# Scales before shifts: the first adaptive layer of a diffusion block is loaded in two halves

## Chip, cores and metric

The kernel runs on one core of a Trainium2 chip. The metric is the time of one launch on the device in microseconds (us), median over runs.

## What is computed

One block over 256 latent tokens and 256 context tokens of width 2048, all in fp32. What matters here is its beginning:

```
mod   = silu(c) @ ada_w + ada_b            # 6 x 2048 columns: sh1, sc1, g1, sh2, sc2, g2; the same for c_ctx
h     = rms_norm(x, norm1_g) * (1 + sc1) + sh1
hc    = rms_norm(ctx, norm1_g) * (1 + csc1) + csh1
proj  = h @ w_in                            # q, k, v of two attentions (8 heads each), then gates
projc = hc @ w_in                           # k, v of the context
```

Two attentions, a gated merge with an output projection and a gated ConvFFN follow; the change leaves them alone, but for the places at which the rest of `ada_w` (columns 4096 and up, 16 groups of 512 columns) is summed beside them.

## The kernel before

**Exact products from rounded halves.** A weight chunk (two 128-row blocks by 512 columns, 512 KB) lands in one of 8 slots of `raw`. ScalarE rounds it into `w_hi` (round_hi, L680), VectorE writes the rest into `w_lo` (split_lo, L1147); both have 4 slots. TensorE multiplies high by high, high by low and low by high (L1811 to L1813 for keys, L1882 to L1885 for q, L1899 to L1901 for v). Activations are stored transposed and split in the same way in `hT`, by 16 column blocks kc. A projection job is 8 slots of 4 tiles; a q job needs latent tokens alone and so fewer columns. Jobs 0 to 5 are k, q, v, q, k, v of the first attention, then comes that attention, then jobs 6 to 11 for the second. A slot can be rounded again once TensorE has used it (`used`), so ScalarE and VectorE can be up to four slots ahead.

**The head.** SP loads, in the order of the list HEAD, 64 chunks of `ada_w` (for one kc, 512 shift and 512 scale columns) in four quarters of 16, and among them the 8 chunks of the first key weights into the `ada_raw` buffers. A unit (unit_ada, L1794) multiplies one such chunk by the pair (c, c_ctx): four fp32 products of 256 columns at four partition offsets (L1803). When a quarter is summed, ScalarE reads the row sums (L746), TensorE turns them into columns (turn_mod, L1783), and VectorE makes gain and shift for four kc (modulation1, L1179). For each kc TensorE turns the normalised tokens (turn_tokens, L1770), ScalarE scales and shifts them in one activation per stream (modulate, L754) and VectorE splits the result (split_modulated, L1201). K_TILES says after which unit each (slot, tile) of the key job, here called a piece, is issued: six products of two kc. Keys of quarter q run behind the units of quarter q + 1, the last two slots after all units. The q job follows (L2010).

**The rest of the adaptive layer.** GpSimd loads 16 groups of 512 columns, 8 chunks of two kc each, into the four `ada_raw` buffers (load_ada, L596). VectorE adds one kc at a time to an accumulator (ada_step, L1208, line L1222). ADA_STEPS says how many of these 256 steps go with which job, ADA_SPAN over which slots; a job's VectorE order is, per slot, the chunk's low half, then the steps. TensorE adds up each group's partitions with four products of 128 columns (sum_mod, L1867, line L1872). Loads of group g, pair p, wait until VectorE has done step 16g + 2(p - 3). The first group waits for `mod1_ready` = 4, that is for the last quarter's gain.

Every engine works its instructions in order. SP's queue, GpSimd's queue and ScalarE's queue are three queues of transfers on the same 16 DMA engines.

Of the kernel before, what the change touches and what calls it, by code (L numbers as in the profile page):

```python
# [23 lines left out]
P = 128  # L24
# [57 lines left out]
K_AFTER = (3, 10)  # L82


K_TILES = {(0, 0): (1, 6), (0, 1): (1, 8), (0, 2): (1, 10), (0, 3): (1, 12),
# [5 lines left out]


def head_units():

    units = [("ada", 0, kc) for kc in range(KC)]
    for q in range(1, QUARTERS):
        for kc in range(KC):
            units += [("k", 2 * q - 2 + n) for n in range(2) if K_AFTER[n] == kc]
            units.append(("ada", q, kc))
    return units + [("k", 2 * QUARTERS - 2), ("k", 2 * QUARTERS - 1)]  # L100
# [3 lines left out]
ADA_UNITS = [unit for unit in HEAD if unit[0] == "ada"]  # L104
ADA_BANKS = (0, 4, 5, 4)
# [3 lines left out]
MOD_BANK = 6  # L109


def loads_before(j):

    return len(ADA_UNITS) // SLOTS + j
# [96 lines left out]
def block_program(nc, x, c, ctx, c_ctx, ada_w, ada_b, norm1_g, w_in, na_rpb, diff_lambda, diff_norm_g,  # L211
# [28 lines left out]
    tokens = place("tokens", arena, [P, 2 * TOK, D])  # L240
    modulated = place("modulated", arena + 32 * kb, [P, 4, 2, SEQ])
# [55 lines left out]
    shift1 = keep("shift1", [P, 2, KC])  # L297
# [31 lines left out]
    with ExitStack() as es:  # L329
# [19 lines left out]
        exp_c_ready = sem("exp_c_ready")  # L349
        start_dve = sem("start_dve")  # L350
        ones_ready = sem("ones_ready")
# [3 lines left out]
        lam_exp = sem("lam_exp")  # L355
        lam_ready = sem("lam_ready")
# [13 lines left out]
        k_landed = sems("k_landed", 2)  # L370
# [144 lines left out]
        def _(sp):  # L515
# [9 lines left out]
            shift_scale = ada_w[0][:, 0:2 * D].rearrange("(k p) (b n) -> p k b n", p=P, b=2)  # L525
            for kind, *unit in HEAD:
                if kind == "ada":
                    q, kc = unit
# [5 lines left out]
                else:  # L534
                    s, = unit
                    if s >= 2:
                        sp.wait_ge(lo_ready[s - 2], 1)
# [1783 lines left out]
```

## Time and profile before

| | us |
|---|---|
| median of 3 runs | 1720.55 (1719.09 to 1721.94) |
| the profiled execution | 1720.02 |
| its span, first to last instruction | 1718.3 |
| TensorE busy, share of span | 1677.8, 98% |
| VectorE, ScalarE busy | 1086.3, 752.6 |

All times in the rows are microseconds from the start of the span, durations too, unless marked ns. PE is TensorE, PEld its weight loads, DVE VectorE, ACT ScalarE, POOL GpSimd, SP SyncE. L1803 is a line of the kernel. PEclk is the granted clock as a share of 2.4 GHz. A product's duration on the timeline overlaps the next; its cost in a stream is the difference of two starts.

### The profile page before, as it was taken

What the parts mean: (1) busy time and instruction counts of PE and PEld (TensorE: products, weight loads), DVE (VectorE), ACT (ScalarE), POOL (GpSimd) and SP (SyncE); (2) the same over time, 40 slices, a digit from 0 to 9 for tenths busy, and PEclk for the clock granted to TensorE, in tenths of its full rate; (3) what the DMA queues carried; (4) which work ended last, traced back from release to release, by engine and by line L of the source; (5) the groups of instructions that cost most, each with busy time, mean ns of one, the idle gap of its engine ahead of it and who ended that gap; (6) DMA issues with size and microseconds to landing.
All of it is one profiled execution on the core that took longest, in us unless ns stands there. A gap on an engine that the chain in (4) does not pass through costs nothing.

```text
span 1718.3 us, 23725 instructions
## 1 busy us (share of the span) xinstructions
PE 1677.8 (98%) x8768; PEld 1371.5 (80%) x8768; DVE 1086.3 (63%) x1366; ACT 752.6 (44%) x962; POOL 108.6 (6%) x161
## 2 busy tenths in 40 slices
PE   4999999999999999999999999999999999999997
PEld 1568888888888678888888788888888888888886
DVE  1338787768887674554555666666666666655556
ACT  2233321623222664444444555555555555544444
POOL 0002222122121000000000000000000000000000
PEclk7999999999999999999999999999999999999999
DMA  9999888269896128566565566666666665655552
GB/s 353 386 387 347 298 296 297 79 215 328 259 321 200 52 90 271 191 189 191 192 234 195 148 190 190 188 191 188 191 187 191 185 184 188 202 195 194 191 193 83
DMA packets 161813, 371.47 MB, mean 216 GB/s; under 512 B 11671, under 2 KB 12423, under 8 KB 160598
## 3 DMA queue, kind: packets, MB, share of 16 engines
q1 hardware_dynamic: 140240, 291.65, 52.5%
q0 software_dynamic: 20144, 74.22, 12.7%
q10 hardware_dynamic: 1366, 4.74, 0.7%
q8 instruction: 41, 0.67, 0.2%
q14 instruction: 22, 0.18, 0.0%
HBM read 368.36 MB, written 2.21 MB: 216 GB/s over the span
## 4 chain that ended last, share of the span: by engine, by line
PE 94%; DMA 3%; DVE 1%; issue 0%; ACT 0%; SPq 0%; DVEq 0%; POOL 0%; ACTq 0%
PE ps L1885 21%; PE ps L1884 11%; PE ps L1899 10%; PE ps L1901 10%; PE ps L1900 10%; PE ps L2253 5%; PE ps L2252 5%; PE ps L2254 5%; PE ps L1811 4%; PE ps L1813 3%; PE ps L1812 3%; DMA raw<-in_ada_w 3%; PE ps L1882 1%; PE ps L1803 1%; PE ps L1968 1%; PE ps L1950 1%
## 5 line engine op out<-in xcount | busy, mean ns | idle before, releaser
L1147 DVE TENSOR_TENSOR w_lo<-raw,w_hi 128x1024 fp32r<-128x1024 f32 x480 | 584.5, 1223 | 419.7 <-ACT w_hi L680 419.2
L680 ACT CAST w_hi<-raw 128x1024 fp32r<-128x1024 f32 x480 | 503.4, 1050 | 763.3 <-PE ps L1885 271.2
L1885 PE MATMUL ps<-h2T,w_hi 128*128 128x512 f32 x1320 | 462.7, 394 | 0.0
L1884 PE MATMUL ps<-h2T,w_lo 128*128 128x256 f32 x1320 | 366.8, 278 | 0.0
L1885 PEld LDWEIGHTS ps<-h2T,w_hi 128*128 128x128 f32 x1320 | 247.8, 188 | 53.7
L1884 PEld LDWEIGHTS ps<-h2T,w_lo 128*128 128x128 f32 x1320 | 248.2, 188 | 3.9
L1899 PE MATMUL ps<-w_hi,hT 128*128 128x512 f32 x512 | 201.7, 394 | 0.0
L1901 PE MATMUL ps<-w_hi,hT 128*128 128x512 f32 x512 | 199.4, 389 | 0.0
L1900 PE MATMUL ps<-w_lo,hT 128*128 128x512 f32 x512 | 199.3, 389 | 0.0
L1222 DVE SCALAR_TENSOR_TENSOR ada_acc<-ada_raw,silu_c,ada_acc 128x512 f32<-128x512 f32 x240 | 179.9, 750 | 29.4 <-DMA ada_raw<-in_ada_w 14.1
L603 POOL DMA_DIRECT2D ada_raw<-in_ada_w x128 | 91.2, 712 | 381.5 <-DVE ada_acc L1222 226.4
L1899 PEld LDWEIGHTS ps<-w_hi,hT 128*128 128x128 f32 x512 | 96.1, 188 | 21.2 <-issue 1.9
L1901 PEld LDWEIGHTS ps<-w_hi,hT 128*128 128x128 f32 x512 | 96.1, 188 | 20.3
L2252 PE MATMUL ps<-w_hi,f_hi 128*128 128x512 f32 x288 | 112.0, 389 | 0.0
L2253 PE MATMUL ps<-w_lo,f_hi 128*128 128x512 f32 x288 | 112.0, 389 | 0.0
L2254 PE MATMUL ps<-w_hi,f_lo 128*128 128x512 f32 x288 | 112.0, 389 | 0.0
L1900 PEld LDWEIGHTS ps<-w_lo,hT 128*128 128x128 f32 x512 | 96.2, 188 | 19.1
L1811 PE MATMUL ps<-hT,w_hi 128*128 128x512 f32 x256 | 103.9, 406 | 1.0 <-DVE hT L1205 1.0
L1813 PE MATMUL ps<-hT,w_lo 128*128 128x512 f32 x256 | 100.0, 390 | 0.0
L1812 PE MATMUL ps<-hT,w_hi 128*128 128x512 f32 x256 | 99.9, 390 | 0.0
L1885 PE MATMUL ps<-hT,w_hi 128*128 128x512 f32 x240 | 84.2, 393 | 0.0
L1884 PE MATMUL ps<-hT,w_lo 128*128 128x256 f32 x240 | 67.3, 280 | 0.0
(231 smaller groups left out, 1985.6 us busy)
## 6 DMA issues: line engine op xcount, KB each, us to landing
raw<-in_ffn_w_up SPq DMA_DIRECT2D x176, 512.0 KB, 3.8
raw<-in_w_in SPq DMA_DIRECT2D x152, 512.0 KB, 4.8
ada_raw<-in_ada_w POOLq DMA_DIRECT2D x128, 512.0 KB, 5.9
raw<-in_ffn_w_down SPq DMA_DIRECT2D x88, 512.0 KB, 4.3
raw<-in_ada_w SPq DMA_DIRECT2D x64, 512.0 KB, 10.4
raw<-in_w_out SPq DMA_DIRECT2D x32, 512.0 KB, 4.4
raw<-in_w_branch_a SPq DMA_DIRECT2D x16, 512.0 KB, 3.6
raw<-in_w_branch_b SPq DMA_DIRECT2D x16, 512.0 KB, 3.6
```

The lines of the kernel that those rows point to most:

```text
L680: act.copy(w_hi[:, s % SPLIT_SLOTS, :], raw[:, s, :]).then_inc(hi_ready[s], 1)
L1147: dve.tensor_tensor(w_lo[:, s % SPLIT_SLOTS, :], raw[:, s, :], w_hi[:, s % SPLIT_SLOTS, :], ALU.subtract).then_inc(lo_ready[s], 1)
L1222: dve.scalar_tensor_tensor(acc, raw_columns, silu_c[:, kc:kc + 1], acc, ALU.mult, ALU.add).then_inc(ada_summed, 1)
L1811: pe.matmul(o, w_hi[:, row4(slot), at], hT[:, :, 0, kc, :], start=(kc == 0), stop=False)
L1884: pe.matmul(ps[:, b + t, 0:SEQ], w_lo[:, row4(s), at], high(kc), start=False, stop=False)
L1885: return pe.matmul(o, w_hi[:, row4(s), at], both(kc), start=False, stop=(kc == KC - 1))
L1899: pe.matmul(ps[:, b, :], hi, w_hi[:, row4(s), at], start=(kc == 0), stop=False)
L1900: pe.matmul(ps[:, b, :], hi, w_lo[:, row4(s), at], start=False, stop=False)
L1901: mm = pe.matmul(ps[:, b, :], lo, w_hi[:, row4(s), at], start=False, stop=(kc == last))
L2252: pe.matmul(ps[:, b, :], hi, w_hi[:, row4(s), at], start=start, stop=False)
L2253: pe.matmul(ps[:, b, :], hi, w_lo[:, row4(s), at], start=False, stop=False)
L2254: return pe.matmul(ps[:, b, :], lo, w_hi[:, row4(s), at], start=False, stop=stop)
```

## The change

Scales and shifts are loaded apart. There are 8 groups of 8 chunks: groups 0 to 3 hold the scales of the four quarters, groups 4 to 7 the shifts; a chunk now holds two kc by 512 columns of one kind, and a unit (unit_mod) is again four products of 256 columns, with the two kc of a chunk at different partition offsets. VectorE therefore adds the two halves when it makes a gain or a shift.

After each scale quarter, ScalarE multiplies the turned tokens by the gain alone and writes them back over `tokens` (scale_tokens); VectorE splits these into `hT` (split_scaled), and keys are computed from scaled tokens without the shift. When a shift group is there, and a key slot has been used, ScalarE adds the shift to the kept scaled tokens and rounds it into `hT` (shift_hi), VectorE writes the low half (shift_lo). The q job (head_q) uses these; its weights too are loaded in the head, through `ada_raw`. Its units of the last two shift groups stand after its slots 1 and 4, the turns after slots 2 and 5.

What the keys lack is shift @ w_k, one vector each for latent and context tokens. GpSimd loads the 8 chunks of key weights a second time (load_fix, into the place of the tokens), each behind one pair of adaptive group 1; after slot 4 of job 2 TensorE waits for all eight and multiplies them by the shifts (fix_products, 64 products of 128 columns), turns the row after slot 6 (turn_fix), and VectorE, after the low half of slot 7, adds the vector to the keys (fix_k) before that slot's adaptive steps. Job 3 waits for `k_bias`.

The token loads move from ScalarE's queue to SP's: x first of all, ctx behind ident, c and c_ctx. The `modulated` buffers go. GpSimd's first adaptive group waits for `hT_ready` = 32, all shifted activations. ADA_STEPS is redrawn: job 1 has none, 112 steps instead of 128 come before the first attention.

```diff
-ADA_STEPS = {1: 12, 2: 34, 3: 13, 4: 37, 5: 32, 6: 24, 7: 13, 8: 28, 9: 13, 10: 32, 11: 18}
+ADA_STEPS = {2: 36, 3: 13, 4: 35, 5: 28, 6: 28, 7: 13, 8: 34, 9: 15, 10: 36, 11: 18}
+MOD_BANKS = (4, 5, 4, 5, 4, 5, 0, 1)
 def head_units():
+    units = []
+    for q in range(QUARTERS):
+        units += [("mod", q, i) for i in range(SLOTS)]
+        units += [("w", 2 * q), ("w", 2 * q + 1)]
+    for q in range(2):
+        units += [("mod", QUARTERS + q, i) for i in range(SLOTS)]
+    units += [("w", SLOTS + n) for n in range(4)]
+    units += [("mod", QUARTERS + 2, i) for i in range(SLOTS)]
+    units += [("w", SLOTS + 4), ("w", SLOTS + 5)]
+    units += [("mod", QUARTERS + 3, i) for i in range(4)]
+    units += [("w", SLOTS + 6)]
+    units += [("mod", QUARTERS + 3, i) for i in range(4, SLOTS)]
+    return units + [("w", SLOTS + 7)]
...
@@ sync
+            sp.dma_start(tokens[:, 0:TOK, :], x[0].rearrange("(t p) n -> p t n", p=P)).then_inc(tokens_landed, 16)
...
+            sp.dma_start(tokens[:, TOK:2 * TOK, :], ctx[0].rearrange("(t p) n -> p t n", p=P))\
+                .then_inc(ctx_landed, 16)
...
+                    if n >= SLOTS:
                         sp.wait_ge(ada1_used, n - SLOTS + 1)
...
+                    if u >= ADA_SLOTS:
+                        sp.wait_ge(lo_ready[(u - ADA_SLOTS) % SLOTS], (u - ADA_SLOTS) // SLOTS + 1)
+                    sp.dma_start(ada_raw[:, u % ADA_SLOTS, :, :], w_in_v[:, 2 * s:2 * s + 2, col:col + GROUP])\
+                        .then_inc(head_landed[u % ADA_SLOTS], 16)
...
@@ gpsimd
-            pool.wait_ge(mod1_ready, QUARTERS)
+            pool.wait_ge(hT_ready, 2 * KC)
             load_ada(0, skip_wait=True)
...
-            pool.wait_ge(hT_ready, KC)
-            load_ada(1, between=load_first_bias)
+            def load_fix(pair):
+                pool.dma_start(fix_w[pair][:].rearrange("p (a n) -> p a n", a=2),
+                               w_in_v[:, 2 * pair:2 * pair + 2, KA:KA + GROUP])\
+                    .then_inc(fix_landed, 16)
+
+            def load_first(pair):
+                load_fix(pair)
+                load_first_bias(pair)
+
+            load_ada(1, between=load_first)
...
@@ scalar (after the scale quarters)
+            read_mod_rows(QUARTERS)
+            head_hi(SLOTS)
+            for kc in range(2):
+                shift_hi(kc)
+            read_mod_rows(QUARTERS + 1)
+            for kc in range(2, 4):
+                shift_hi(kc)
+            head_hi(SLOTS + 1)
+            for kc in range(4, 6):
+                shift_hi(kc)
+            read_result(JOB_NA)
+            for kc in range(6, 8):
+                shift_hi(kc)
+            head_hi(SLOTS + 2)
+            head_hi(SLOTS + 3)
+            read_mod_rows(QUARTERS + 2)
+            head_hi(SLOTS + 4)
+            for kc in range(8, 10):
+                shift_hi(kc)
+            head_hi(SLOTS + 5)
+            for kc in range(10, 12):
+                shift_hi(kc)
+            read_mod_rows(QUARTERS + 3)
+            for kc in range(12, 14):
+                shift_hi(kc)
+            head_hi(SLOTS + 6)
+            for kc in range(14, KC):
+                shift_hi(kc)
+            head_hi(SLOTS + 7)
...
@@ vector
+            def fix_k():
+                dve.wait_ge(mod_cols_ready, MOD_GROUPS + 1)
+                turned = ps[:, FIX_TURNED_BANK, 0:P].rearrange("p (a w) -> p a w", w=32)
+                dve.tensor_copy(k_bias[:], turned[:, :, 0:2]).then_inc(mod1_ready, 1)
+                dve.wait_ge(mod1_ready, MOD_GROUPS + 1)
+                dve.wait_ge(kv_read, 1)
+                keys = kT[:, 0:TILES, :].rearrange("p a (s n) -> p a s n", s=2)
+                dve.tensor_tensor(keys, keys, k_bias[:].unsqueeze(3).to_broadcast([P, TILES, 2, SEQ]), ALU.add)\
                     .then_inc(mod1_ready, 1)
...
+                    split_lo(j, s)
+                    if (j, s) == (FIX_JOB, SLOTS - 1):
+                        fix_k()
...
@@ tensor
+            for i in range(SLOTS):
+                unit_mod(0, i)
+            turn_tokens(0)
+            turn_mod(0)
+            turn_tokens(1)
+            pe.wait_ge(vecs_ready, 3)
+            for q in range(QUARTERS - 1):
+                for n in range(2 * TILES):
+                    s, t = 2 * q + n // TILES, n % TILES
+                    head_k(s, t)
+                    if n in (0, 1):
+                        turn_tokens(SHARE * q + 2 + n)
+                    if n < 4:
+                        unit_mod(q + 1, 2 * n)
+                        unit_mod(q + 1, 2 * n + 1)
+                    if n == 3:
+                        turn_tokens(SHARE * (q + 1))
+                    if n == 4:
+                        turn_mod(q + 1)
+                    if n == 5:
+                        turn_tokens(SHARE * (q + 1) + 1)
+            for n in range(2 * TILES):
+                s, t = SLOTS - 2 + n // TILES, n % TILES
+                head_k(s, t)
+                if n in (0, 1):
+                    turn_tokens(KC - 2 + n)
+                    for i in range(4):
+                        unit_mod(QUARTERS, 4 * n + i)
+                if n == 2:
+                    turn_mod(QUARTERS)
+                if n in (3, 4):
+                    for i in range(4):
+                        unit_mod(QUARTERS + 1, 4 * (n - 3) + i)
+                if n == 6:
+                    turn_mod(QUARTERS + 1)
...
+            for s in range(SLOTS):
+                head_q(s)
+                if s in (1, 4):
+                    for i in range(SLOTS):
+                        unit_mod(QUARTERS + (2 if s == 1 else 3), i)
+                if s == 2:
+                    turn_mod(QUARTERS + 2)
+                if s == 5:
+                    turn_mod(QUARTERS + 3)
...
+            def fix_between(s, t):
+                if (s, t) == (4, TILES - 1):
+                    fix_products()
+                if (s, t) == (6, TILES - 1):
+                    turn_fix()
+
+            projection(FIX_JOB, fix_between)
+            pe.wait_ge(mod1_ready, MOD_GROUPS + 1)
+            for j in range(FIX_JOB + 1, JOB_DIFF - 1):
                 projection(j)
```

## Rows read from the trace of the kernel before

**Rows 1.** The page: busy us, share of the span and instructions of each engine.

```profile
PE 1677.8 (98%) x8768; PEld 1371.5 (80%) x8768; DVE 1086.3 (63%) x1366; ACT 752.6 (44%) x962; POOL 108.6 (6%) x161
```

**Rows 2.** Busy us (count) by stretch; PEclk, DMA share and GB/s last.

```profile
0.00:34.00 34.00, 13.35 (x103) 0.77 0.94 344
34.00:52.00 18.00, 15.12 (x114) 0.59 1.05 387
...
52.00:112.00 60.00, 59.81 (x472) 33.54 (x469) 16.83 (x29) 14.26 (x24) 0.00 (x0) 0.99 1.05 387
...
131.00:153.00 22.00, 22.00 (x127) 19.21 (x126) 19.68 (x24) 10.15 (x9) 7.05 (x10) 1.00 1.02 349
...
164.00:174.00 10.00, 10.00 (x51) 7.86 (x51) 9.25 (x12) 2.11 (x2) 3.10 (x5) 1.00 0.94 324
```

**Rows 3.** TensorE's longest wait, 52 to 132 us (us in total, times, longest).

```profile
PE ps L1811 <- DVE hT L1205: 1.0, 1, 1.0
```

**Rows 4.** Timeline, TensorE: first product of keys, of jobs 1, 2 and 3.

```profile
52.13 0.80 PE L1811 MATMUL ps<-hT,w_hi 128*128 128x512 f32 x1
...
131.87 0.39 PE L1882 MATMUL ps<-hT,w_hi 128*128 128x512 f32 x1
...
154.06 0.39 PE L1899 MATMUL ps<-w_hi,hT 128*128 128x512 f32 x1
...
198.76 0.39 PE L1882 MATMUL ps<-hT,w_hi 128*128 128x512 f32 x1
```

**Rows 5.** Timeline, TensorE: sums and key pieces in turn, 54 to 65 us.

```profile
54.01 1.07 PE L1803 MATMUL ps<-raw,c_pair 128*32 128x256 f32 x16
...
61.78 0.64 PE L1803 MATMUL ps<-raw,c_pair 128*32 128x256 f32 x8
...
63.94 0.64 PE L1803 MATMUL ps<-raw,c_pair 128*32 128x256 f32 x8
64.51 0.66 PE L1779 MATMUL ps<-consts,tokens 128*128 128x128 f32 x4
```

**Rows 6.** Groups by form and timeline, V job, 154 to 199 us.

```profile
L1222 DVE SCALAR_TENSOR_TENSOR ada_acc<-ada_raw,silu_c,ada_acc 128x512 f32<-128x512 f32 x30 | 22.5, 750 | 5.2 <-DMA ada_raw<-in_ada_w 3.5
...
L1147 DVE TENSOR_TENSOR w_lo<-raw,w_hi 128x1024 fp32r<-128x1024 f32 x9 | 11.0, 1220 | 3.4 <-ACT w_hi L680 3.4
L680 ACT CAST w_hi<-raw 128x1024 fp32r<-128x1024 f32 x8 | 8.4, 1054 | 27.6 <-PE ps L1901 25.9 <-PE ps L1885 1.7
L1234 DVE TENSOR_TENSOR qT<-qT,ps 128x1024 f32<-128x1024 f32 x1 | 1.2, 1212 | 0.0
...
163.23 4.17 DVE L1222 SCALAR_TENSOR_TENSOR ada_acc<-ada_raw,silu_c,ada_acc 128x512 f32<-128x512 f32 x5
```

**Rows 7.** Timeline: the last two normalisations.

```profile
28.89 2.48 DVE L1257 TENSOR_SCALAR tokens<-tokens,rms 128x2048 f32<-128x2048 f32 x2
```

**Rows 8.** TensorE: busy us, count and granted clock by stretch, 44 to 54 us.

```profile
45.00:46.00 1.00, 0.36 (x8) 1.00 1.05 385
46.00:47.00 1.00, 0.43 (x9) 0.50 1.04 383
...
53.00:54.00 1.00, 1.00 (x5) 1.00 1.10 395
```

**Rows 9.** Tile ada_raw, 100 to 200 us: GpSimd's loads, issue to landing.

```profile
DMA to landing us min/median/max: 4.9/7.0/10.4
```

**Rows 10.** Timeline, TensorE: four sums of 128 columns between key products.

```profile
243.09 0.39 PE L1813 MATMUL ps<-hT,w_lo 128*128 128x512 f32 x1
243.41 0.43 PE L1872 MATMUL ps<-ada_acc,exp_c 128*32 128x128 f32 x8
243.77 0.50 PE L1811 MATMUL ps<-hT,w_hi 128*128 128x512 f32 x1
```

**Rows 11.** VectorE's waits after the first attention, 355 to 600 us.

```profile
DVE w_lo L1147 <- ACT w_hi L680: 13.1, 7, 2.9
```

**Rows 12.** Timeline: the two activations of one kc.

```profile
68.01 1.02 ACT L760 ACTIVATE modulated<-ps,shift,gain 128x256 f32<-128x256 f32 x2 [1.83 <-DVE gain L1198]
```

More of the change, by code:

```diff
@@ new lines, in shift_hi @@
+            def shift_hi(kc):
+                act.wait_ge(mod1_ready, QUARTERS + kc // SHARE + 1)
+                act.wait_ge(hT_ready, kc + 1)
+                act.wait_ge(used[kc // 2], 1)
+                for st in range(2):
+                    ins = act.activation(hT[:, st, 0, kc, :].rearrange("p (t n) -> p t n", t=TOK),
+                                         tokens[:, st * TOK:(st + 1) * TOK, kc * P:(kc + 1) * P], ACT.Identity,
+                                         bias=shift_pair[:, 2 * kc + st:2 * kc + st + 1])
+                ins.then_inc(hT_hi_ready, 1)
@@ L831, in _ @@
             last = JOB_DIFF - 1
-            for j in range(JOB_NA + 1, JOB_DIFF):
+            for j in range(JOB_NA + 2, JOB_DIFF):
                 for s in range(SLOTS):
@@ L1162, in step @@
                 dve.wait_ge(start_dve, steps)
[L1165 removed]
+            step(dve.memset(ones[:], 1.0))
             step(dve.memset(epsilon[:], EPS))
             step(dve.memset(c_pair[:], 0.0))
+            step(dve.memset(shift_pair[:], 0.0))
             dve.wait_ge(vecs_turned, 1)
@@ new lines, in modulation1, with scaled @@
+                dve.wait_ge(mod1_step, (2 * g if gain else QUARTERS + g) + 1)
+                ins = dve.tensor_tensor(by_piece(into), sums[:, 1, 0:2], by_piece(into), ALU.add)
+                if gain:
+                    ins.then_inc(mod1_step, 1)
+                    dve.wait_ge(mod1_step, 2 * g + 2)
+                    ins = dve.scalar_tensor_tensor(into, into, 1.0, spread(V_N1), ALU.add, ALU.mult)
+                ins.then_inc(mod1_ready, 1)
+            def scaled(st, kc):
+                return tokens[:, st * TOK:(st + 1) * TOK, kc * P:(kc + 1) * P]
@@ new lines, in by_tile, with split_scaled @@
+            def by_tile(v):
+                return v.rearrange("p (t n) -> p t n", t=TOK)
+            def split_scaled(kc):
+                dve.wait_ge(modulated_ready, 2 * kc + 2)
+                both = tokens[:, :, kc * P:(kc + 1) * P].rearrange("p (s t) n -> p s t n", s=2)
+                hi, lo = (hT[:, :, part, kc, :].rearrange("p s (t n) -> p s t n", t=TOK) for part in range(2))
+                dve.tensor_copy(hi, both).then_inc(hT_hi_ready, 1)
+                dve.wait_ge(hT_hi_ready, kc + 1)
+                dve.tensor_tensor(lo, both, hi, ALU.subtract).then_inc(hT_ready, 1)
@@ L1337, in _ @@
             last = JOB_DIFF - 1
-            for j in range(JOB_NA + 1, JOB_DIFF):
+            for j in range(JOB_NA + 2, JOB_DIFF):
                 for s in range(SLOTS):
@@ new lines, in fix_products @@
+            def fix_products():
+                pe.wait_ge(*results_read(JOB_NA + 1))
+                pe.wait_ge(fix_landed, 16 * SLOTS)
+                for kc in range(KC):
+                    pair, r = divmod(kc, 2)
+                    for a, at in enumerate(PIECE_AT):
+                        col = r * GROUP + a * P
+                        mm = pe.matmul(ps[at:at + 32, FIX_BANK, 0:P], shift_pair[:, 2 * kc:2 * kc + 32],
+                                       fix_w[pair][:, col:col + P], start=(kc == 0), stop=(kc == KC - 1))
+                mm.then_inc(ada1_used, 1)
```

322 lines of the change are left out of this document (165 added, 157 removed), and 5 rows, old and new, of the table K_TILES.

## Prediction

> **What bounds the kernel now.** The page comes first [rows 1]: TensorE is busy 98% of the span. So there is something to win only in a stage where it idles, and work added to it later costs its full length. The second view is the busy time by stretch [rows 2]: up to 34 us TensorE has 13.4 us of work; from 34 to 52 us it is granted a mean clock of 0.59, a mix of its levels of 1.2 and 2.4 GHz; meanwhile DMA moves 344 and 387 GB/s. From 52 us on TensorE is full. The third view, its waits from 52 to 132 us [rows 3], has one of 1.0 us at its head and little else. Loads run at 387 GB/s all that time, 1.355 us for a chunk of 512 KB, yet they are just fast enough. The marks of before, by first product [rows 4]: keys 52.1, q job 131.9, V job 154.1, next job 198.8 us.
>
> The change can win what TensorE does earlier than 52 us, some 18 us at most. Whether it keeps that is decided in the q and V jobs, so they are walked below.
>
> **Prices.** Two units of the adaptive sums are busy 1.07 us, one 0.64 [rows 5]: a unit more is 0.43. One unit and a key piece take 2.16 from start to start; less 0.43 and six products at 0.23 (1.38), changing kind and back is 0.35. A transpose group is busy 0.66 [rows 5] and overlaps its neighbours; I count 0.5. A weight chunk takes 1.05 on ScalarE and 1.22 on VectorE (1.18 from start to start); an adaptive step 0.83 in a row of five [rows 6].
>
> **Start.** The tokens go from ScalarE's queue to the head of SP's. Before, the last normalisation ended at 31.4 [rows 7]. Counting 387 GB/s from 3.8 us, both are there by 16. c, now behind x, comes 4 us later; this holds up the exponent, not the squares that follow it by more than 0.5. The squares of ctx no longer wait for it: normalised at 28.0. Tokens, small rows and eight scale chunks are 9.0 MB: landed at 27.0. Then transpose, read, turn to 29.7; gain 30.4; two scaled groups, their splits and one weight half, 3.6: first key piece at **34.0**.
>
> **Keys.** A quarter is 8 pieces (11.0), 8 units with four changes (4.8), four transpose groups and a turn (2.2): 18.0. The last one has 16 units and two transpose groups: 20.9. Ten chunks need only 13.6 of DMA, so TensorE sets this pace and the loads wait for its slots. The clock: before, it fell to 0.50 at 46 us, after 2 us in which TensorE was little busy, and was 1.00 again at 53, after six us of work [rows 8]; I charge 2.4, somewhat under half of them. 34.0 + 2.4 + 3 x 18.0 + 20.9 = 111.3. The turn of the second shift group waits for a ScalarE read behind two shifts and the chunk that lands at 107.9: +2.0, keys end at **113.3**, 18.6 ahead of 131.9. But 16 of the units that before were done by then are still to come (7 us).
>
> **q job.** Its work is 22.2 us [rows 4], 2.77 a slot. Now loads are late: the second shift group is issued only as the first is consumed, from 93.3. Counting a latency of 2 us, the n-th chunk after that lands at 95.3 + 1.355n. q0 and q1 end at 118.9; the third group's last chunk (n = 20) lands at 122.4, its sums end at 122.9; q2, q3 to 128.8; q4 waits 1.1 for its shift and ends at 132.7; the last group's last chunk (n = 31) lands at 137.3, sums to 137.8; q5 to 140.6. Then a serial chain with nothing else for TensorE to do: turn 0.4, shift vector 0.7, four ScalarE shifts 2.0, chunk 14 on ScalarE 1.1 and on VectorE 1.2: q6 starts at 146.0 after 5.4 idle. By [rows 8] it runs slow, +2.5: V job at **154.1**. What was won is given back, term **0.0**. All shifted activations are ready at 147.8.
>
> **V job.** GpSimd's adaptive loads wait for that 147.8. Their shortest way from issue to landing is 4.9 [rows 9], so VectorE starts steps at 152.7. Ten steps (8.3) and two chunks: 163.4. Fourteen more (11.6), three chunks (3.5) and the q addition 1.2: the 24th at 179.7. The second group's eight pairs wait for steps 10, 12 to 24, and each is followed on the queue by one of the eight chunks of key weights that are loaded again. The eighth goes out at 181 and lands at 186 at best. But between, DMA is asked for 16 chunks by GpSimd and 3 by SP. A chunk costs 1.355 at 387 GB/s and 1.62 at 324 [rows 2]; I take 349 GB/s, 1.50, the stretch in which both queues are filled as here. 165.0 + 19 x 1.50 + 0.5 for bias rows = **194.0**. TensorE stands at the wait for all eight at 154.1 + 5 x 5.44 = 181.3: **+12.7** (4.7 by issue alone, 15.0 by 1.62).
>
> A rule weighed: the Trainium skill ("DMA: Bandwidth & Descriptors", Bandwidth) lists 425 GB/s for a large load. By an estimate from it the eighth chunk would land at 188.9 and the term be 7.6; the 387 traced with one queue and 324 and 349 with two [rows 2] are lower, and decide.
>
> The fix's products: the nearest row, four sums of 128 columns, opens 0.68 us between two key products that else follow in 0.23 [rows 10]. Less the change of kind that is 0.22 for 128 columns, half a unit: 16 x 0.22 + 0.4 = **+3.9** (at most 5.8, at 0.36). After 12 us idle the clock is low: **+2.3** (0 to 2.8). Turn: +0.4. VectorE then waits, V's last chunk done, for that turn one slot (5.4) before the job's end, and still has the copy 0.2, the key addition 2 x 1.21 [rows 6], five steps 4.1 and the next job's first chunk 1.2: 8.1, so TensorE waits **+2.7** (0 to 4).
>
> **Later and at nothing.** Adaptive steps stay 256; 16 move behind the first attention, 12 us of VectorE. VectorE waits 13.1 us there for chunks that ScalarE can't round before TensorE frees their slot [rows 11]: it is slots ahead, and this lead is the cover; without it I allow +3, a quarter of the 12. Scaling and shifting apart doubles these passes (ScalarE 1.02 for one kc [rows 12], VectorE about as much): 16 us on each, and they are busy 14 and 17 of the 60 us to 112 [rows 2], on the path only where named.
>
> **Sum.** 0.0 + 12.7 + 3.9 + 2.3 + 0.4 + 2.7 = +22.0. The profiled execution took 1720.0 (span 1718.3, median of the runs 1720.55): **1742**.
>
> **Rivals.** (a) DMA keeps up and issue alone binds: 8 less, **1734**. For it: in the V job before VectorE waited only 3.5 us for adaptive data [rows 6]. Against: eight chunks fewer were asked for, at 324 GB/s already.
> (b) The other side, **faster**: TensorE is never starved. The work from 52.1 to 154.1 (102), plus 14.5 units, two transpose groups, four turns, 2.4 of slow clock, less half of the 24 changes of kind, all from 34.0, puts V at 142.5, and the key weights come in time: 142.5 + 44.7 + 3.9 + 0.4 + 2.7 = 194.2 for 198.8, **1715.5**. It decides once V begins before 147 and the eighth chunk is there 27 us later. Against: 24 steps come 32 us after the last shift, whatever DMA does. For: no wait of that size showed up before.
> (c) The clock stays up in the gaps: 2.3 less, **1739.7**; the earlier V job only lengthens the wait, which hangs on 147.8.
> (d) VectorE's lead is gone after the first attention: 3 more, **1745**.
>
> **How the numbers follow.** Forecast 0.42, (c) 0.12, (d) 0.12, (a) 0.18, (b) 0.10; 0.06 for a mixture of (a) and (b), 0.05 of it within 0.2% (3.4 us, what a measurement of this kernel can tell from no change). The range goes down to 1726, 8 below (a) for the walk of the head, and up to 1750: chunks at 1.62 (+2.3), fix at 5.8 (+1.9), lead gone (+3). Left out: (b), the mixture's most and some above. Faster 0.10, same 0.05, slower 0.85.
>
> **What would show it.** Right: keys from about 34, q job from 113, idle near 141 to 146, V job at about 154; one idle of some 12 us after V's slot 4, ended by the second load of the key weights; the next job at about 220; equal lengths from there. Wrong: a V job before 147, or no idle in it. An idle of 5 us there is (a).

## The result, and the profile after

| | before | after |
|---|---|---|
| median of the runs, us | 1720.72 (6 runs, 1719.09 to 1721.94) | 1751.21 (6 runs, 1750.70 to 1752.32) |
| profiled execution, its span | 1720.02, 1718.3 | 1751.53, 1749.7 |

The ratio is 1.0178 (95%: 1.0165 to 1.0191): 30.5 us slower where 22 were forecast, and 1.2 above the end of the range. The page has TensorE's busy time nearly where it was [rows 1], so the loss is waiting, not work:

```profile
PE 1675.7 (96%) x8905; PEld 1380.2 (79%) x8905; DVE 1102.7 (63%) x1409; ACT 763.3 (44%) x999; POOL 114.1 (7%) x169
```

The four marks of [rows 4], and behind them TensorE's waits from 30 to 290 us (us in total, times, longest), which answer to [rows 3]:

```profile
39.14 0.76 PE L1946 MATMUL ps<-hT,w_hi 128*128 128x512 f32 x1 [2.22 <-DVE hT L1269]
...
117.34 0.39 PE L2026 MATMUL ps<-hT,w_hi 128*128 128x512 f32 x1
...
158.39 0.39 PE L2043 MATMUL ps<-w_hi,hT 128*128 128x512 f32 x1
...
227.59 0.47 PE L2026 MATMUL ps<-hT,w_hi 128*128 128x512 f32 x1 [1.95 <-DVE w_lo L1197]
```

```profile
PE ps L1931 <- DMA fix_w<-in_w_in: 17.4, 1, 17.4
PE ps L2028 <- DVE w_lo L1202: 4.5, 1, 4.5
PE ps L1888 <- DVE tokens L1339: 4.3, 1, 4.3
PE ps L1919 <- DMA raw<-in_ada_w: 4.2, 5, 1.6
...
PE ps L2026 <- DVE w_lo L1197: 1.9, 1, 1.9
```

Against before the keys start 13.0 us earlier and the q job 14.5, the V job 4.3 later, job 3 28.8 later. The 14.5 are lost, and more, inside the q job; inside the V job 24.5 go, 17.4 of them in one wait for the key weights that are loaded again. From job 3 to the end another 2.6 are lost.

**The start.** Timeline of TensorE, VectorE and ScalarE up to 34 us; the last row answers to [rows 7]:

```profile
17.95 0.45 PE L1968 MATMUL ps<-consts,param_rows 128*128 128x128 f32 x1 [5.61 <-DMA param_rows<-in_diff_norm_g]
...
19.17 0.66 DVE L1343 COPY vecs<-ps 128x480 f32<-128x480 f32 x1 [4.98 <-PE ps L1973]
...
20.41 0.20 ACT L808 ACTIVATE lam<-lam 128x2 f32<-128x2 f32 x1 [7.49 <-DVE lam L1350]
...
22.03 1.89 ACT L745 ACTIVATE junk<-tokens 128x2048 f32<-128x2048 f32 x1
...
31.16 2.48 DVE L1339 TENSOR_SCALAR tokens<-tokens,rms 128x2048 f32<-128x2048 f32 x2
```

The parameter rows come at 17.95 (11.51 before); the 4 MB of tokens now run on SP's queue beside them, with x ahead of c, and no run takes the two apart. VectorE copies them, then reduces the second attention's lambda; ScalarE waits for that reduction with its exponential (L808), and the squares stand behind it in ScalarE's order. The last normalisation ends at 33.6. Busy time by stretch, as in [rows 2]:

```profile
0.00:34.00 34.00, 10.38 (x73) 3.04 (x74) 8.64 (x27) 12.81 (x18) 2.39 (x9) 1.00 0.96 343
34.00:52.00 18.00, 15.12 (x107) 9.66 (x106) 8.23 (x14) 5.23 (x10) 0.00 (x0) 1.00 0.98 341
52.00:112.00 60.00, 58.40 (x462) 40.03 (x462) 20.95 (x40) 16.26 (x33) 0.00 (x0) 1.00 0.83 291
131.00:153.00 22.00, 15.73 (x125) 11.31 (x124) 11.43 (x24) 10.86 (x22) 0.46 (x1) 0.89 0.98 358
```

In the third row DMA moves 291 GB/s where it moved 387. TensorE takes chunks more slowly than they could land, and at 93 to 97 us DMA stands quite still:

```profile
93.00:97.00 4.00, 4.00 (x36) 2.99 (x38) 1.76 (x2) 1.21 (x3) 0.00 (x0) 1.00 0.00 0
```

Up to 154 us the kernel before had moved a mean of 371 GB/s, this one 330: 57.1 and 50.8 MB. Of the 6.3 MB between them 5.4 are GpSimd's: its queue had moved 5.7 MB by then (12 adaptive chunks issued) and now 0.2 (3 issued, the first at 152.5), because its first group waits for all shifted activations. The V job then asks GpSimd for 26 chunks, 18 adaptive ones and 8 of key weights, where it was 17 before, and moves 18.3 MB where it was 14.8. So what it moves more is less than the key weights (4.2 MB); but it begins with a single adaptive chunk landed (VectorE's first step is at 157.3).

**The q job's end.** VectorE, ScalarE and TensorE after the last turn (146.00 us), then the stretches behind it:

```profile
146.57 0.17 DVE L1250 TENSOR_TENSOR shift_pair<-ps,shift_pair 128x8 f32<-128x8 f32 x1
...
146.77 1.70 ACT L778 ACTIVATE hT<-tokens,shift_pair 128x256 fp32r<-128x256 f32 x4 [3.19 <-DVE shift_pair L1250]
148.38 1.03 ACT L695 CAST w_hi<-ada_raw 128x1024 fp32r<-128x1024 f32 x1
...
149.44 1.23 DVE L1202 TENSOR_TENSOR w_lo<-ada_raw,w_hi 128x1024 fp32r<-128x1024 f32 x1
...
150.81 0.55 PE L2028 MATMUL ps<-hT,w_lo 128*128 128x256 f32 x1 [4.48 <-DVE w_lo L1202]
```

```profile
148.00:150.00 2.00, 0.00 (x0) 0.00 (x0) 1.95 (x5) 2.00 (x5) 0.00 (x0) 0.56 1.06 388
150.00:152.00 2.00, 1.19 (x4) 1.12 (x5) 2.00 (x5) 2.00 (x5) 0.00 (x0) 0.50 0.42 144
152.00:154.00 2.00, 2.00 (x7) 1.71 (x7) 2.00 (x3) 1.85 (x2) 1.46 (x3) 0.50 0.80 257
154.00:156.00 2.00, 2.00 (x10) 1.68 (x10) 0.52 (x1) 0.12 (x1) 1.41 (x2) 0.73 0.88 243
```

This is the serial chain of the forecast, 4.48 us of idle time, and the granted clock is at the 1.2 GHz level for the products behind it.

**The V job.** VectorE's steps and GpSimd's last load of key weights, then TensorE at the products for the shift vector and behind them; last, issue to landing of the eight loads, and the stretches around:

```profile
183.71 1.61 DVE L1304 SCALAR_TENSOR_TENSOR ada_acc<-ada_raw,silu_c,ada_acc 128x512 f32<-128x512 f32 x2 [3.38 <-DMA ada_raw<-in_ada_w]
...
187.69 1.61 DVE L1304 SCALAR_TENSOR_TENSOR ada_acc<-ada_raw,silu_c,ada_acc 128x512 f32<-128x512 f32 x2 [1.24 <-DMA ada_raw<-in_ada_w]
...
190.30 0.72 POOL L635 DMA_DIRECT2D fix_w<-in_w_in  x1
...
203.17 1.25 PE L1931 MATMUL ps<-fix_w,shift_pair 128*32 128x128 f32 x17 [17.41 <-DMA fix_w<-in_w_in]
...
208.29 0.50 PE L2043 MATMUL ps<-w_hi,hT 128*128 128x512 f32 x1
```

```profile
DMA to landing us min/median/max: 6.7/12.4/14.5
...
188.00:203.00 15.00, 0.00 (x0) 0.00 (x0) 7.50 (x10) 0.00 (x0) 3.54 (x5) 0.54 1.03 386
203.00:205.00 2.00, 1.83 (x36) 1.86 (x40) 0.00 (x0) 0.00 (x0) 0.00 (x0) 0.50 1.02 384
205.00:207.00 2.00, 2.00 (x60) 2.00 (x55) 0.00 (x0) 0.00 (x0) 0.00 (x0) 0.68 0.24 90
```

DMA works at 386 GB/s for the whole of the wait. VectorE, whose steps free the slots behind which the key weights stand, itself waits for chunks: each side of GpSimd's queue holds up the other.

**Behind it**, VectorE and the key addition, ahead of the wait of 1.95 us at 227.59:

```profile
220.19 0.17 DVE L1283 COPY k_bias<-ps 128x8 f32<-128x8 f32 x1 [9.29 <-PE ps L1939]
220.39 2.29 DVE L1287 TENSOR_TENSOR kT<-kT,k_bias 128x2048 f32<-128x2048 f32 x1
...
226.23 1.22 DVE L1197 TENSOR_TENSOR w_lo<-raw,w_hi 128x1024 fp32r<-128x1024 f32 x1
```

### The profile page after: what moved, and what is told of

Same layout as the page of the kernel before. It is cut to its first block, busy times and chain, and to the rows that moved or that the text cites. A ratio compares the mean times of both kernels' runs of the same rounds, so it can differ in the third digit from the quotient of the medians.

```text
span 1749.7 us, 24123 instructions
## 1 busy us (share of the span) xinstructions
PE 1675.7 (96%) x8905; PEld 1380.2 (79%) x8905; DVE 1102.7 (63%) x1409; ACT 763.3 (44%) x999; POOL 114.1 (7%) x169
## 3 DMA queue, kind: packets, MB, share of 16 engines
q0 software_dynamic: 21296, 78.42, 13.1%
## 4 chain that ended last, share of the span: by engine, by line
PE 84%; DMA 6%; DVE 5%; issue 2%; ACT 1%; SPq 0%; ACTq 0%; POOL 0%; DVEq 0%; POOLq 0%
PE ps L2029 19%; PE ps L2028 9%; PE ps L2043 8%; PE ps L2045 8%; PE ps L2044 8%; PE ps L2427 5%; PE ps L2428 5%; PE ps L2429 4%; PE ps L1946 3%; PE ps L1948 3%; PE ps L1947 3%; DMA ada_raw<-in_ada_w 3%; DVE ada_acc L1304 2%; DMA raw<-in_ada_w 2%; PE ps L2026 1%
## 5 line engine op out<-in xcount | busy, mean ns | idle before, releaser
L1197 DVE TENSOR_TENSOR w_lo<-raw,w_hi 128x1024 fp32r<-128x1024 f32 x472 | 574.8, 1223 | 408.3 <-ACT w_hi L688 408.3
L688 ACT CAST w_hi<-raw 128x1024 fp32r<-128x1024 f32 x472 | 495.1, 1050 | 755.1 <-PE ps L2029 268.8
```

Source lines behind the costliest of these rows:

```text
L688: act.copy(w_hi[:, s % SPLIT_SLOTS, :], raw[:, s, :]).then_inc(hi_ready[s], 1)
L1197: dve.tensor_tensor(w_lo[:, s % SPLIT_SLOTS, :], raw[:, s, :], w_hi[:, s % SPLIT_SLOTS, :], ALU.subtract).then_inc(lo_ready[s], 1)
```

## The experiments

Theory A is that of the forecast: the V job's wait for key weights is the main loss. The rivals are the head, the chain at the q job's end, VectorE's order, and one cause beneath all of them, the demand on DMA in the V job. "First attention" is its first weight load. Values of one execution are meant where no interval stands. Six kernels with the changed kernel's head (after, e1, e2, e5, e10, e12) start the V job at 158.4 to 160.1 us, so a shift of that mark by under 2 us in one profile says little. The times of e1, e2 and e4 to e8 are single runs; the six runs of the changed kernel spread over 1.6 us and the seven of e9 over 5.3, so a difference of 1 us between two kernels isn't clear of noise.

| kernel | time | keys | q job | V job | job 3 | first attention |
|---|---|---|---|---|---|---|
| before | 1720.7 | 52.1 | 131.9 | 154.1 | 198.8 | 299.8 |
| after | 1751.2 | 39.1 | 117.3 | 158.4 | 227.6 | 330.2 |
| e1, key weights first | 1742.6 | 39.4 | 118.2 | 160.0 | 217.7 | 320.8 |
| e2, a quarter of them | 1744.8 | 39.3 | 117.5 | 159.0 | 220.3 | 323.1 |
| e4, weights before shifts | 1750.2 | 39.5 | 120.0 | 158.8 | 227.4 | 330.2 |
| e5, steps before the addition | 1749.0 | 39.0 | 118.0 | 160.1 | 227.2 | 328.7 |
| e6, chunks before shifts | 1751.3 | 39.2 | 119.7 | 158.3 | 229.6 | 332.1 |
| e7, squares first | 1750.6 | 34.9 | 114.1 | 157.2 | 226.2 | 330.9 |
| e10, e1 and e5 | 1738.4 | 39.3 | 117.7 | 159.4 | 217.5 | 318.8 |
| e8, e1, e5, e6 and e7 | 1732.8 | 35.0 | 113.8 | 153.5 | 210.3 | 311.4 |
| e12, e1 and fewer steps | 1732.0 | 39.0 | 118.2 | 160.0 | 208.6 | 310.4 |
| e9, e8 and fewer steps | 1724.6 | 34.9 | 114.0 | 155.0 | 202.5 | 304.1 |
| e11, e9 and an early turn | 1723.5 | 34.7 | 113.9 | 152.8 | 201.6 | 303.2 |
| e13, e11 with 1/16 of the fix | 1719.6 | 34.8 | 113.9 | 152.8 | 201.2 | 302.8 |

**e1: the key weights earlier on GpSimd's queue.**

```diff
-            load_ada(0, skip_wait=True)
+            load_ada(0, skip_wait=True, between=load_fix)
...
-            load_ada(1, between=load_first)
+            load_ada(1, between=load_first_bias)
```

> The changed kernel with one edit: GpSimd issues the eight chunks of key weights between the pairs of adaptive group 0 instead of group 1, so the eighth waits for step 8, not for step 24. Theory A (the wait of 17.4 us stands on when the chunks are issued, together with the DMA backlog in front of them): the eighth chunk goes out at about 163 us and lands near 180, TensorE does not wait for the key weights at all, but the adaptive data of group 0 come half as fast, so VectorE is late with the low halves and TensorE waits some 5 to 9 us for those instead; the time falls by 8 to 13 us against the changed kernel. Theory B (the sheer bytes set the end of the stage, whatever their order): TensorE's waits in the V job sum to the same 17 us and the time stays within 2 us.

The wait for key weights is gone and job 3 starts 9.9 us earlier; 8.6 us faster. The 17.4 did not all come back: three new waits of TensorE stand in the V job, for weight halves that VectorE makes late because it stands at adaptive steps:

```profile
PE ps L2043 <- DVE w_lo L1197: 4.8, 3, 2.4
```

**e2: a quarter of each key-weight load.** Only the first tile's columns are loaded, and used for all four tiles.

```diff
-                pool.dma_start(fix_w[pair][:].rearrange("p (a n) -> p a n", a=2),
-                               w_in_v[:, 2 * pair:2 * pair + 2, KA:KA + GROUP])
+                pool.dma_start(fix_w[pair][:].rearrange("p (a n) -> p a n", a=2)[:, :, 0:P],
+                               w_in_v[:, 2 * pair:2 * pair + 2, KA:KA + P])
...
-                        col = r * GROUP + a * P
+                        col = r * GROUP
```

> The changed kernel, but each of the eight key-weight chunks loads only its first 128 of 512 columns (128 KB instead of 512 KB) and the fix multiplies these for all four tiles; so the keys' shift is right for the first tile alone. Order and waits of all loads are as before. Theory A (backlog): 3.1 MB less, 8 us of DMA at 387 GB/s; VectorE no longer waits for adaptive data, step 24 comes near 185 instead of 192, the eighth chunk lands at 191 to 193 instead of 203, TensorE's wait falls from 17.4 to 5 to 8 us, the time by 9 to 12. Theory C (the issue alone, behind step 24, sets it and bandwidth hardly counts): the wait falls by under 3 us.

```profile
PE ps L1931 <- DMA fix_w<-in_w_in: 8.1, 1, 8.1
```

The wait falls by 9.3 us for 3.1 MB less, 8.7 us at the 362 GB/s of the stretch from 169 to 203 us. The order of the queue was left alone, so it is bytes that this part of the wait is made of; issue and VectorE's steps can make at most the 8.1 that are left. Bytes act twice: the last of these loads goes out at 187.7 and not 190.3, since VectorE waits less for its chunks, and the rest of the gain is a shorter time to landing. The time gains 6.4 of the 9.3, less than the 9 to 12 that theory A had.

**e4: the order on SP's queue.** Weight chunks 8 to 11 stand before the second shift group, to fill DMA's gap at 93 us.

```diff
-    for q in range(2):
-        units += [("mod", QUARTERS + q, i) for i in range(SLOTS)]
+    units += [("mod", QUARTERS, i) for i in range(SLOTS)]
     units += [("w", SLOTS + n) for n in range(4)]
+    units += [("mod", QUARTERS + 1, i) for i in range(SLOTS)]
```

> The changed kernel with the four q weight chunks w8 to w11 loaded before the second shift group instead of behind it. In the changed kernel DMA stands still for about 5 us near 93 us, since the second shift group waits for slots that TensorE frees only then. Theory A (q job is bound by the arrival of the last shift chunks): the four chunks fill that gap, the third and last shift groups land 4 to 5 us earlier, the V job begins 3 to 5 us earlier than 158.4 and the end moves by the same. Rival D (q job is bound by the serial chain of turn, shift and round): the V job begins at most 1 us earlier.

DMA's idle time moved to 125 to 128 us, where SP now stands at a load whose slot isn't free, and the V job starts where it did. The gap at 93 us is not the cause by itself: whatever the order, each slot is freed by TensorE. The chain behind the last turn (146.01) has its 4.48 us of idle time here too, as rival D had it.

**e5: VectorE's order.** The key addition behind the adaptive steps of its slot.

```diff
-                    if (j, s) == (FIX_JOB, SLOTS - 1):
-                        fix_k()
                     if s == 3:
                         read_result(j - 1)
                     ada_steps(j, s)
+                    if (j, s) == (FIX_JOB, SLOTS - 1):
+                        fix_k()
```

> The changed kernel with VectorE's fix of the keys put behind the five adaptive steps of job 2, slot 7, instead of ahead of them. VectorE waits 9.3 us for the turned row there, in which the steps fit. Theory: the chain from the turn to job 3's first low half shortens by 4.1 us, TensorE's wait of 1.9 us at the head of job 3 goes away, VectorE enters the following jobs with 2 us more lead; the time falls by 2 to 4 us. Rival: the 3.4 us lost between job 3 and the second attention come from elsewhere, then it falls by no more than 2.

TensorE's wait of 1.95 us at job 3 is gone, and from job 3 to the second attention 365.3 us pass as before (365.0) and not 368.4. The run gains 2.2, and lies 1.7 under the fastest of the changed kernel; its V job happened to start 1.7 later. So most of the loss behind job 3 was VectorE's order too.

**e6: the q job's chain.**

```diff
             read_mod_rows(QUARTERS + 3)
-            for kc in range(12, 14):
+            head_hi(SLOTS + 6)
+            head_hi(SLOTS + 7)
+            for kc in range(12, KC):
                 shift_hi(kc)
-            head_hi(SLOTS + 6)
-            for kc in range(14, KC):
-                shift_hi(kc)
-            head_hi(SLOTS + 7)
```

and the same on VectorE, there ahead of the shift vector too.

> The last two weight chunks of the query job (14 and 15) are converted before the last four shifts instead of between and behind them; nothing else changes. Serial-chain theory: the V job starts at 158.4 because the last shift group's turned sums arrive at 146.0 and then four ScalarE shifts, one ScalarE conversion (1.1) and one VectorE subtraction (1.2) stand in line. Then the V job's first product comes 1.2 to 2.4 us earlier (156.0 to 157.2), and the run takes 1748.8 to 1750 us. Rival, issue theory: ScalarE's and VectorE's work of this stretch hides behind the TensorE's own backlog and slow clock, and what is won is given back in the V job's wait for key weights, since DMA sets that: first product of the V job anywhere, query projection of job 3 at 227.6 and the time 1751 unchanged.

From the last turn to the V job 11.1 us pass and not 12.4, as the chain theory had it, but this execution's sums came 1.1 late, and the V job's wait for key weights grew to 18.7. In the time, nothing (one run): the rival's forecast held.

**e7: the start.**

```diff
-            act.wait_ge(lam_step, 2)
-            act.activation(lam[:], lam[:], ACT.Exp).then_inc(exp_ready, 1)
+            act.wait_ge(exp_ready, 1)
             warm_up(ACT.Sqrt)
```

The exponential then stands in job 5, the two steps on lambda ahead of job 6, and the normalisation of x before the copy of the parameter rows.

> The exponential of the differential attention's lambda and the two steps behind it are moved out of the head (to before the first attention and before the seventh job), and VectorE normalises the tokens of x before it copies the turned parameter rows. So the squares no longer wait for the parameter rows that land at 17.95 us. Head theory (the late rows cost 5 us at the start, and TensorE's order carries that to the V job): first square at about 14.4 instead of 22.0, last normalisation done at about 26, then the first group's scales (last product with c at 29.4) set the start: first key product at 34.5 to 35.5 instead of 39.1, V job's first product 3.5 to 4.6 us earlier than 158.4, and the time 1746 to 1748 us. Rival, DMA theory: the order and rate of the 28 MB ahead of the V job set its start, whatever the head does: first key product moves, V job's first product stays within 1 us of 158.4, and the time stays at 1750 to 1752 us.

ScalarE's first square, and TensorE's last three sums of the last shift group with the turn behind them:

```profile
14.58 1.89 ACT L745 ACTIVATE junk<-tokens 128x2048 f32<-128x2048 f32 x1
```

```profile
137.58 0.64 PE L1920 MATMUL ps<-raw,c_pair 128*32 128x256 f32 x8 [0.72 <-DMA raw<-in_ada_w]
138.91 0.64 PE L1920 MATMUL ps<-raw,c_pair 128*32 128x256 f32 x8 [0.69 <-DMA raw<-in_ada_w]
140.28 1.08 PE L1920 MATMUL ps<-raw,c_pair 128*32 128x256 f32 x8 [0.73 <-DMA raw<-in_ada_w]
...
145.17 0.33 PE L1904 MATMUL ps<-consts,mod_rows 98*128 98x98 f32 x2
```

Keys start 4.2 us earlier and the q job 3.2, but the turn only 0.8. The clock fell to the lower level at 140 to 143 us, behind 4 us in which TensorE had 2.1 us of sums to do (the unit at 140.28 takes 1.08 where the two before it took 0.64). From this last unit to the turn 4.9 us pass, and 3.5 in the changed kernel: 1.4 of the 2.4 us that are lost on the way. The time gains 0.7, within the noise of single runs. Neither theory had this right: the head does set when the q job starts, yet what it gives is lost again before the V job. The squares were the forecast's error and hardly its cost.

**e10 and e8: do the terms add?**

> Only the two moves of the key fix together: its weights loaded with the first adaptive group, its VectorE work behind the adaptive steps. Separate theory: each cures a wait of its own (8.6 for the weights, 2.2 for VectorE's order, from the single runs), so 1751.2 - 10.8 = 1740.4, expected 1739 to 1742 us; then the head's and the query job's moves, which alone gave 0.7 and -0.1, are worth 8 us as soon as the wait for key weights is gone, since they bring the V job forward by 4.9. Rival: the two fix moves give more together than alone (1733 to 1737), and the head moves are worth next to nothing in any company.

> Four moves at once: key weights for the added vector loaded with the first group of adaptive weights, the key fix behind the adaptive steps of its slot, the last two chunks converted before the last shifts, and the squares first. If the terms are separate (wait for key weights 8.6, VectorE's order 2.2, serial chain 1 to 2, head 3.5 to 4.6), the run takes 1733 to 1737 us, still over the 1720.7 of the kernel before, and the V job starts at 153 to 156. If they share one cause, the adaptive weights' DMA, the gains don't add: an earlier V job meets the same landings, the wait for key weights or for adaptive chunks grows in its place, and the time is 1739 to 1742 us.

e10's ratio to before is 1.0109 (1.0092 to 1.0126), 12.8 us under the changed kernel where 10.8 were the sum. On top of it e6 and e7, worth 0.6 us alone, bring the V job from 159.4 to 153.5 us and the time down by 5.6 more. That is the single run of e8 against the median of four; e9 and e12 below bear it out, since e9, which has e5, e6 and e7 on top of e12, lies 7.5 under it by the medians of seven and four runs and 6.4 by the ratios, and e5 alone gave 2.2. The granted clock from 146 to 152 us is 1.00 in e8 (0.81 in e10), behind a wait of 3.1 us. It had fallen before that, as in e7: 0.50 at 140 to 142 us, behind thin sums.

```profile
146.00:152.00 6.00, 4.14 (x24) 3.68 (x25) 4.50 (x9) 5.38 (x10) 2.31 (x4) 1.00 0.87 297
```

But the V job is 56.8 us long against 44.7, only 3.6 of that for the added products, and TensorE waits in it for VectorE, which waits for DMA:

```profile
PE ps L2040 <- DVE w_lo L1196: 5.8, 4, 2.0
```

**e12 and e9: fewer bytes in the V job.**

```diff
-ADA_STEPS = {2: 36, 3: 13, 4: 35, 5: 28, 6: 28, 7: 13, 8: 34, 9: 15, 10: 36, 11: 18}
+ADA_STEPS = {2: 24, 3: 17, 4: 39, 5: 32, 6: 28, 7: 13, 8: 34, 9: 15, 10: 36, 11: 18}
```

> Two moves on the changed kernel: the key weights loaded with the first adaptive group, and the adaptive steps of jobs 2 to 5 shared out as 24, 17, 39, 32. Head and query job are the changed kernel's. With the key weights in the second group this share isn't possible: 24 steps don't free the slots behind which the last key-weight chunks stand, so the first move is what allows the second. Demand theory: the V job's bytes are what cost (36 steps are 18 chunks of 0.5 MB, and 8 of key weights beside them), so 12 steps fewer give some 8 us here as they did in the kernel with all moves (8.2): V job to job 3 in 47 to 51 us instead of 57.7, time 1733 to 1736 us against 1742.6 with the first move alone. Rival, order theory: fewer steps helped there only because the V job had been freed by the other moves; here 1738 to 1742 us.

> The kernel with all four moves (1732.8), and the adaptive steps of jobs 2 to 5 shared out as 24, 17, 39, 32 instead of 36, 13, 35, 28 (112 in both). Theory: what is left of the loss is the V job, 56.8 us to job 3 where it was 44.7 before: some 5 for the fix products, 5.8 of waits for weight halves that VectorE makes late because it stands at adaptive steps whose chunks the DMA brings late behind the key weights. With 12 steps fewer, 6 chunks of 0.5 MB less are needed there: V job to job 3 in 50 to 53 us, and the time 1727 to 1730 us. Rival: the DMA backlog only moves on into jobs 3 to 5, with the same bytes before the first attention: V job shorter, first attention at 311 as in that kernel, time 1731 to 1734 us.

With 12 steps (6 chunks, 3.1 MB) moved to jobs 3 to 5, the V job is 48.7 us (e12) and 47.5 us (e9) long, TensorE doesn't wait in it, and job 3 to the first attention stays at 101.8 and 101.6 us (102.6 in the changed kernel): the backlog doesn't move on. (In e12 0.7 us are waited at the head of job 3.) e12 is at 1.0063 of before (1.0048 to 1.0078), 10.6 us under e1; e9 at 1.0026 (1.0014 to 1.0037), 8.2 under e8. Both gains are at or above what the demand theory had (8 us in e12, 1727 to 1730 us for e9), and the rivals are out. But the edit takes two things out of the V job: 3.1 MB, and 12 of VectorE's steps, some 10 us at 0.83 each. No run parts them. From 160 to 200 us DMA moves 369 GB/s in e1 and 368 in e12, and VectorE waits for chunks 15.3 us in the one and 16.0 in the other; what differs is that fewer such steps stand ahead of each low half. Only e2 varies the bytes alone. TensorE at the added products in e9, and the first product behind them:

```profile
182.26 3.70 PE L1928 MATMUL ps<-fix_w,shift_pair 128*32 128x128 f32 x128
185.89 0.50 PE L2040 MATMUL ps<-w_hi,hT 128*128 128x512 f32 x1
```

**e11: the last shift group turned earlier.**

```diff
                 for t in range(TILES):
                     mm = unit_paired(s, t, 4, ...)
-                mm.then_inc(used[s], 1)
+                    if t == TILES - 1:
+                        mm.then_inc(used[s], 1)
+                    if (s, t) == (5, 1):
+                        turn_mod(QUARTERS + 3)
...
-                if s == 5:
-                    turn_mod(QUARTERS + 3)
```

> The kernel with all moves and fewer steps (1724.6), and the last shift group turned after half of the products of the sixth weight chunk instead of behind all of them, with the low half of the last chunk made behind two of the four last shifts. Serial-chain theory: TensorE's idle time before the seventh chunk falls from 3.6 to 2 to 3 us, the V job starts at 151 to 153.5 us instead of 155.0, and since the granted clock is 0.50 for the stretch behind a long idle time, a shorter one may keep it at 1.00: time 1720.5 to 1723 us, about the kernel before (1719.4), at best 1 us below it. Rival: the V job's chunks land when they did, so that an earlier start meets DMA waits: time within 1 us of 1724.6.

TensorE's idle time falls from 3.6 to 2.4 us and the V job starts 2.2 earlier, as expected, but a wait of 0.9 appears in it, and job 3 starts 0.9 earlier. The time is 1.0 under e9, its ratio 1.0019 (1.0010 to 1.0028) beside e9's 1.0026 (1.0014 to 1.0037): the intervals overlap, so a gain in the time isn't shown. Both theories had a part. The clock fell here all the same (0.51 at 148 to 150 us).

**e13: what the fix costs once nothing waits for it.**

> The kernel with the early turn (1723.5), of the keys' shift only the first of 16 chunks of the inner dimension is computed: 1 of 8 key-weight loads and 8 of 128 products, so the kernel leaves out 15 sixteenths of that vector. Inherent-price theory: what is left against the kernel before (3.4 us) is TensorE's time for the 128 small products, about 4.7 at full clock, and no wait: 1718.5 to 1720 us. DMA theory: 3.7 MB of loads fewer bring more than the products, since VectorE's adaptive steps in the V job wait 15.6 us for chunks: 1712 to 1717 us. If the products cost nothing beside the load (they fill TensorE's waiting time): 1722 to 1724 us.

1719.64 us, ratio 0.9997 (0.9988 to 1.0007): 3.9 us under e11, which had 3.4 left to the kernel before. So without nearly all of the fix the kernel is level with the one before, as the inherent-price theory forecast. Its "no wait" failed:

```profile
PE ps L2044 <- DVE w_lo L1198: 2.4, 1, 2.4
```

The products left out are 3.3 us of TensorE (between the V products around them lie 0.68 us here, 3.95 in e9). But this execution has a wait of 2.4 us in the V job (0.9 in e11) and behind it a clock of 0.66 from 160 to 165 us, and both job 3 and the first attention start only 0.4 earlier than in e11; the spans differ by 2.3. So how the 3.9 divide between products, loads and waits isn't shown, and a share of DMA isn't ruled out. No kernel of the series is faster than the one before.

## Why the prediction was off

The direction and the course were right: keys early, the gain given back in the q job by a serial chain, one long wait in the V job after slot 4, and equal lengths from there but for 2.6 us. The size was short, step by step:

- **Start** (forecast 34.0, measured 39.1). The step "this holds up the exponent, not the squares that follow it by more than 0.5" failed. I had followed c, and not the parameter rows and the second exponential behind them: first square at 22.0 and not about 16. By e7 this is worth 4.2 us at the first key, but 0.7 in the time.
- **Keys.** The pace held: 78.2 us from first key to q job, 79.3 forecast, with the 2.4 for a low clock in it. The first products do start 0.43 us apart (39.70, 40.13, 40.55) where those from 44 us on start 0.23 apart, although the row of the granted clock shows 1.00 there.
- **q job.** Its length held (41.1 for 40.8), its idle time too (4.5 for 5.4), and the low clock. So the V job's term was +4.3 and not 0.0, all of it brought along from the start. e7 shows that the term wouldn't have been 0 with a right start either: the V job starts at 157.2, with a second fall of the clock in the way (1.4 us). Only the four moves together reach 153.5.
- **The wait** (forecast 12.7, measured 17.4). This is the term that was mis-sized most, and the step that failed is VectorE's walk to its 24th step. TensorE came 4.5 us later than forecast (185.8 for 181.3), the eighth chunk 9.2 later (203.2 for 194.0). All of the 9.2 lies ahead of its issue, at 190.3 and not 181; from issue to landing 12.9 us pass, 13 by the forecast. VectorE's first step came 4.6 late (157.3 for 152.7), which is the late start again. I put the 24th at 179.7 by its own durations and let it wait for nothing on the way, and it waited 6.5 us for chunks (1.45, 0.39, 3.38 and 1.24) and ended at 189.3. Meanwhile 12.3 MB or 23.5 chunks' worth went through from 169 to 203 us, at 1.45 us each, where I counted 19 at 1.50: the price of a chunk was right and the number too low, by 2.7 on GpSimd's queue (9.8 MB) and 1.9 on SP's (2.6 MB). In rival (a)'s argument I used the 3.5 us that VectorE had waited before as evidence for, though these were the sign that the stretch had no room. e2 shows that bytes set at least 9.3 us of the wait, e12 that 12 steps less with their 3.1 MB are worth 10.6 us once the key weights come early.
- **Fix and clock** (3.9 + 2.3, measured 5.1). At full clock the products take 3.6 (e9); the idle time ahead costs 1.5 more.
- **VectorE after the turn** (2.7, measured 1.95; the parts that I gave as 8.1 add up to 7.9, so 2.5), and **later at nothing**, measured 2.6. The last failed in part: rival (d) had its sign and size, but not its cause. VectorE's lead wasn't lost behind the attention by the 16 moved steps, but at job 3 by the key addition (2.29 us) and five steps ahead of the next low half; e5 brings it back.
- **The rule weighed.** The wait passed at 386 GB/s, with two queues asked for all they could give; no stretch of 10 us or more that I read shows over 389. The Trainium skill ("DMA: Bandwidth & Descriptors", Bandwidth) lists 425 for a load of 16 MB, by which the term came out at 7.6; this trace of 512 KB loads doesn't agree.

Two figures of the walk don't follow from its prices. The 165.0 from which the 19 chunks are counted isn't derived: the steps before it end at 163.4, from which the term would have been 11.1 and not 12.7 (the second group began to go out at 169.3). And rival (b)'s 142.5 comes out at 143.0.

Summed: V job +4.3, wait 17.4, products with clock 5.1, VectorE 1.95, later 2.6 give 31.4, the difference of the spans. The 22.0 fell short by 4.3, 4.7 and 2.6, while the fix with its turn and VectorE behind it were 2.3 too dear.

Not tried: a V job with the key weights kept on chip from their first load, which would save the second load; no room for them was looked for. Nor was an earlier condition for GpSimd's first adaptive group, which is what leaves the V job almost without adaptive data at its start; how much that costs by itself is open.

## What to carry to other kernels

Work that needs a second load is paid for in the stage that makes the load, whatever was won before it: here 26 chunks were asked of GpSimd's queue in a job that had asked it for 17, and TensorE paid with a wait. Loads held back until later data are ready (0.2 MB by 154 us where there had been 5.7) leave the next stage little to begin with. Count the bytes that each stage is asked for, not only the work on its engines, and read a small wait for DMA on an engine that isn't critical as the sign that there is no room left. When one wait hides others, moves that show no gain alone (0.1 us slower and 0.7 faster, in single runs) can be worth 4 to 6 together once it is gone; test them again in that company before they are dropped. And where an earlier move allows a better share (12 steps fewer in the V job), the share can be worth more than the move.

## What was unexpected of the hardware

TensorE's granted clock turns small shifts of timing into larger ones. In the changed kernel it stood at 0.50 to 0.73 from 150 to 156 us behind an idle time of 4.5 us; behind 3.1 us in e8 it stayed at 1.00, behind 2.4 us in e11 it fell to 0.51. In e7 it fell with no long idle time at all, only behind thin sums (2.1 us of work in 4), and so it did in e8 ahead of the 3.1 us. So the length of one gap alone didn't decide it in these runs; what does is left open. From the last turn to the V job 12.1 to 13.1 us pass in the seven kernels with the same chain (after, e1, e2, e4, e5, e10, e12), all with the same 4.48 us of idle time, so where the low clock falls is worth up to 1 us there. It isn't all: e5's V job started 1.7 late because of a wait of 2.2 us for a chunk at 129.75. Why the runs of e9 lie between 1721.6 and 1727.0 us no trace shows.
